# Decode attention of a two-layer decoder: softmax and values in two halves of four samples inside the prompt's heads

## The reference

```
def shared_kv(s, g, w_kv, b_f):
    z = rmsnorm(s, g) @ w_kv
    k = z[..., :SEQ_WIDTH].reshape(bsz, t, FOX_HEADS, HEAD_DIM)
    v = z[..., SEQ_WIDTH:2 * SEQ_WIDTH].reshape(bsz, t, FOX_HEADS, HEAD_DIM)
    logf = jax.nn.log_sigmoid(z[..., 2 * SEQ_WIDTH:].astype(F32) + b_f.astype(F32)).astype(s.dtype)
    return k, v, logf
...
def fox_block(q, k, v, cq, ck, qpos, kpos):
    s = jnp.einsum('bqhd,bkhd->bhqk', q, k).astype(F32) * ATTN_SCALE
    s = s + jnp.transpose(cq, (0, 2, 1))[..., None] - jnp.transpose(ck, (0, 2, 1))[:, :, None, :]
    s = jnp.where(mask, s, NEG_INF)
    p = jax.nn.softmax(s, axis=-1).astype(v.dtype)
    return jnp.einsum('bhqk,bkhd->bqhd', p, v)
...
def fox_sample(q, k_new, v_new, logf_new, k_past, v_past, logf_past):
    k = jnp.concatenate([k_past, k_new.astype(k_past.dtype)], axis=1)
    v = jnp.concatenate([v_past, v_new.astype(v_past.dtype)], axis=1)
    logf = jnp.concatenate([logf_past.astype(F32), logf_new.astype(F32)], axis=1)
    c = jnp.cumsum(logf, axis=1)
    return fox_block(q, k, v, c[:, past:], c, kpos[past:], kpos)
```

## Time and profile before

| | |
|---|---|
| median of 3 runs | 1623.56 us |
| lowest and highest | 1621.72 and 1624.8 us |
| the profiled execution | 1620.65 us |
| its span on the core | 1618.9 us |
| mean granted TensorE clock | 0.937 |
| PE busy | 1440.2 us (89%) |
| DVE, ACT, POOL busy | 983.1, 615.6, 671.6 us |

### The profile page before, as it was taken

How to read it: one execution, slowest core, us unless ns; L and a number is a source line. 1 busy time by engine, 2 the same in 40 slices (tenths; PEclk the granted TensorE clock), 3 DMA queues, 4 the chain that set the end, 5 groups by cost and what they waited for, 6 DMA issues and landing times.

```text
span 1618.9 us, 32326 instructions
## 1 busy us (share of the span) xinstructions
PE 1440.2 (89%) x12076; PEld 1331.4 (82%) x12076; DVE 983.1 (61%) x1553; ACT 615.6 (38%) x1004; POOL 671.6 (41%) x429
## 2 busy tenths in 40 slices
PE   7985597879998999999878979997979998999996
PEld 6974477879998999999777966644979998999996
DVE  5768826566775057763647468751577771277755
ACT  4552435245662133422332216520355551233312
POOL 0685421323343344442366769301414433344430
PEclk9997758999999999999898989997989999999998
DMA  5334452222323223333224746797212332233321
GB/s 168 120 92 80 84 153 77 66 66 79 81 80 93 83 88 91 96 92 84 75 81 142 207 151 201 234 373 249 85 46 78 90 93 83 73 90 92 109 78 58
DMA packets 288134, 180.42 MB, mean 111 GB/s; under 512 B 54072, under 2 KB 272860, under 8 KB 287980
## 3 DMA queue, kind: packets, MB, share of 16 engines
...
...
## 4 chain that ended last, share of the span: by engine, by line
PE 52%; DVE 17%; issue 16%; POOL 6%; ACT 4%; DVEq 1%; SPq 1%; DMA 1%; ACTq 0%; POOLq 0%
PE big L2414 42%; ACT yc L2279 3%; PE misc L2483 2%; PE misc L2469 2%; DVE rstd L1116 1%; PE big L2717 1%; DVE hf L1688 1%; POOL s5s L881 1%; DVE x_lo L1147 1%; DVE uc L1673 1%; DVE yc L1683 1%; DVE y L1605 1%; POOL e_tmp L881 1%; DVE yc L1680 1%; DVE tmp L1157 1%
## 5 line engine op out<-in xcount | busy, mean ns | idle before, releaser
L877 POOL TENSOR_TENSOR w_lo<-raw,w_hi 128x1024 fp32r<-128x1024 f32 (+2 forms) x163 | 423.0, 2595 | 787.9 <-ACT w_hi L1963 787.7
L2414 PE MATMUL big<-x_hi,w_hi 128*128 128x264 f32 (+1 forms) x2184 | 457.9, 292 | 41.2 <-DVE x_lo L1147 24.2
L2414 PE MATMUL big<-x_hi,w_lo 128*128 128x264 f32 (+1 forms) x2184 | 444.9, 285 | 0.0
L2414 PE MATMUL big<-x_lo,w_hi 128*128 128x264 f32 (+1 forms) x2184 | 443.7, 285 | 0.0
L1963 ACT ACTIVATE w_hi<-raw 128x1024 fp32r<-128x1024 f32 (+2 forms) x179 | 198.3, 1108 | 537.6 <-PE big L2414 497.9
L2414 PEld LDWEIGHTS big<-x_hi,w_hi 128*128 128x128 f32 x2184 | 342.4, 191 | 52.9 <-issue 44.2
L2414 PEld LDWEIGHTS big<-x_lo,w_hi 128*128 128x128 f32 x2184 | 340.9, 191 | 0.0
L2414 PEld LDWEIGHTS big<-x_hi,w_lo 128*128 128x128 f32 x2184 | 340.4, 191 | 0.0
L1677 DVE SCALAR_TENSOR_TENSOR yc<-uc,convw,yc 128x512 f32<-128x512 f32 x88 | 106.3, 1208 | 114.3 <-ACT yc L2279 114.3
L2414 PE MATMUL big<-h_hi,w_hi 128*128 128x264 f32 x704 | 144.7, 287 | 15.2 <-DVE h_lo L1692 12.0
L2414 PE MATMUL big<-h_lo,w_hi 128*128 128x264 f32 x704 | 143.0, 285 | 0.0
...
## 6 DMA issues: line engine op xcount, KB each, us to landing
...
areas<-in_cache_k SPq DMA_DIRECT2D x49, 384.0 KB, 4.1
areas<-in_cache_v SPq DMA_DIRECT2D x35, 384.0 KB, 6.2
...
extra<-in_cache_v SPq DMA_DIRECT2D x19, 384.0 KB, 5.3
...
```

What stands on the lines that cost most here:

```text
L877: pool.tensor_tensor(w_lo[slot][:, 0:kb, :], raw[slot][:, 0:kb, :], w_hi[slot][:, 0:kb, :].bitcast(F32), ALU.subtract).then_inc(lo_made, 1)
L2414: ins = pe.matmul(big[2 * slot + b_][:, 0:c1 - c0], w[slot][:, k, :], r[:, c0:c1], start=(k == 0 and n_ == 0), stop=(k == kb - 1 and n_ == 2))
```

## The change

1. **Two halves.** The scores, the sums of the softmax and the softmax itself are split into samples 0 to 3 and 4 to 7. The first half's softmax stands at steps 2 to 6, the second's at 30 to 34. The 16 pairs of pages of samples 0 to 3 have their value products one pair at a time, at steps 7, 8, 10, 12, 14, 15, 17, 19, 21, 22, 24, 26, 28, 29, 31 and 33. The value pages of samples 4 to 7 stay in the late part.
2. **Page order.** `page_loads` lets key and value pages take turns from the ninth key page after the thirtieth on. The key reductions are spread over 30 steps. The block of stores and mk still stands behind the last key page. mv moves back by eight value pages.
3. **Tables.** LOGF_AT, DECAY_AT from 1, 3 to 2, 4; K_FIRST (2, 3), one reduction of them ahead of the second norm; queries of samples 5, 6, 7 at steps 4, 12, 19.
4. **Log-forget chain.** One instruction in place of minus and min; the chain's second part (`log_forget`) stands behind kvT of panel 0, the scan, which now subtracts (`decay_row`), behind kvT of panel 1.
5. **POOL beside x's split.** Three key products ahead of the first w_lo; the fourth waits until x_lo is made.
6. **Masks.** `diagonal` stands after key product 31, its tiles in other memory.
7. `win1_queries`: the spreads of samples 0 and 1 move from the last slice of panel 6 to slices 0 and 2 of panel 7.

```diff
-Q_STEP = {5: 1, 6: 6, 7: 12}
-LOGF_AT, DECAY_AT = 1, 3
-K_STEP = 7 / 5
-K_FIRST = (3, 5)
-K_BEFORE_LO = (2, 5, 7, 9, 11, 13, 15, 17, 19, 21, 23, 25)
-K_BEHIND = K_BEFORE_LO[2:] + (27, 29)
-SOFT_AT = 25
-PV_AT = (30, 31, 32, 33, 34, 36, 38, 39)
-PV_BESIDE = len(PV_AT) // 2
+Q_STEP = {5: 4, 6: 12, 7: 19}
+LOGF_AT, DECAY_AT = 2, 4
+SPLITS_KV = 4 * KD + 3 * KS
+K_FIRST = (2, 3)
+K_BEFORE_LO = (3, 4, 6, 8, 10, 12, 14, 16, 18, 20, 22, 24)
+K_BEHIND = K_BEFORE_LO[2:] + (26, 28)
+SOFT_AT = (2, 30)
+PV_AT = tuple(7 + 7 * i // 4 for i in range(16))
+PV_BESIDE = len(PV_AT) // 4
...
+    early, ks, vs = (0, 1, 2, 3, KV_PAGE), (0, 1, 2, 3, AREAS[5]), AREAS[0:5]
+    out = [(n, early[n % 5]) for n in range(K_EARLY)]
+    nk, nv, turn = K_EARLY, 0, 0
+    while nk < NB * PAGES:
+        if nk < K_EARLY + 8 or turn:
+            out.append((nk, ks[(nk - K_EARLY) % 5]))
+            nk, turn = nk + 1, 0
+        else:
+            out.append((NB * PAGES + nv, vs[nv % 5]))
+            nv, turn = nv + 1, 1
...
 def scores_read(n):
-    return min(NB * PAGES, K_EARLY + int(K_STEP * n))
+    last = SOFT_AT[1]
+    return K_EARLY + min(n, last) * (NB * PAGES - K_EARLY) // last
...
-            for n in range(K_EARLY, v_at):
+            for n, _ in PAGE_LOADS[K_EARLY:LAST_KEYS + 1]:
                 page_load(n)
             for c in range(4):
                 store(O["prompt_v"][0, c * P:(c + 1) * P], vtok[:, c, :, 0:DH])
...
-            for n in range(v_at, 2 * NB * PAGES):
+            for n, _ in PAGE_LOADS[LAST_KEYS + 1:]:
                 page_load(n)
-                if n == 3 * NB * PAGES // 2:
+                if n == 13 * NB * PAGES // 8:
                     mem_v(1, mb[1])
...
                     for i in range(n):
+                        if i == 1:
+                            pool.wait_ge(s_("xlo_made"), SPLITS_KV)
                         k_products(K_BEFORE_LO[i - 1] if i else 0, K_BEFORE_LO[i])
                         lo(base + i, (base + i) % 2, kb)
-                    k_products(K_BEFORE_LO[n - 1], NB * PAGES)
+                    k_products(K_BEFORE_LO[n - 1], K_EARLY + 2)
                     diagonal()
+                    k_products(K_EARLY + 2, NB * PAGES)
...
-                tt(sc[0:NB, :, PAGES, :], idb, snew.unsqueeze(1).to_broadcast([NB, NB, HEADS]), ALU.mult)
-                tt(sc[0:NB, :, PAGES, :], sc[0:NB, :, PAGES, :], idneg.unsqueeze(2).to_broadcast([NB, NB, HEADS]), ALU.add)
+                for i in range(2):
+                    bs = slice(HALF_B * i, HALF_B * i + HALF_B)
+                    idb = ident[0:NB, bs].unsqueeze(2).to_broadcast([NB, HALF_B, HEADS])
+                    tt(sc[i][0:NB, :, PAGES, :], idb, snew.unsqueeze(1).to_broadcast([NB, HALF_B, HEADS]), ALU.mult)
+                    tt(sc[i][0:NB, :, PAGES, :], sc[i][0:NB, :, PAGES, :],
+                       idneg[:, bs].unsqueeze(2).to_broadcast([NB, HALF_B, HEADS]), ALU.add)
...
-            ts(m_, z_, -1.0, None, ALU.mult, ALU.bypass)
-            tell(V.tensor_tensor(m_, m_, z_, ALU.min), s_("nabs_ready"), 1)
-            dve.wait_ge(s_("log_made"), 1)
-            tell(V.scalar_tensor_tensor(m_, z_, 0.0, l_, ALU.min, ALU.subtract), s_("lf_ready"), 1)
-            sync()
-            do(V.memset(z_, 1.0))
-            sync()
-            do(V.tensor_tensor_scan(l_[:, 0:T], z_[:, 0:T], m_[:, 0:T], 0.0, ALU.mult, ALU.add))
-            sync()
-            do(V.tensor_scalar(lf[:, 0, 0:T], l_[:, 0:T], -1.0, None, ALU.mult, ALU.bypass))
+            tell(V.scalar_tensor_tensor(m_, z_, -1.0, z_, ALU.mult, ALU.min), s_("nabs_ready"), 1)
+
+            def log_forget():
+
+                dve.wait_ge(s_("log_made"), 1)
+                tell(V.scalar_tensor_tensor(m_, z_, 0.0, l_, ALU.min, ALU.subtract), s_("lf_ready"), 1)
+                sync()
+                do(V.memset(l_, 1.0))
+
+            def decay_row():
+
+                do(V.tensor_tensor_scan(z_[:, 0:T], l_[:, 0:T], m_[:, 0:T], 0.0, ALU.mult, ALU.subtract))
...
                 read_panel(q, lambda n, c0, c1: kvT[:, c0:c1])
                 sync()
                 mark(s_("kvT_ready"))
+                if m == 0:
+                    log_forget()
+                elif m == 1:
+                    decay_row()
                 k_scores(K_BEHIND[m])
```

More of the change, by code:

```diff
@@ L182, with page_loads @@
 Q_PANEL = {2: 2, 3: 5, 4: 9}
-Q_STEP = {5: 1, 6: 6, 7: 12}
-LOGF_AT, DECAY_AT = 1, 3
-K_STEP = 7 / 5
-K_FIRST = (3, 5)
-K_BEFORE_LO = (2, 5, 7, 9, 11, 13, 15, 17, 19, 21, 23, 25)
-K_BEHIND = K_BEFORE_LO[2:] + (27, 29)
-SOFT_AT = 25
-PV_AT = (30, 31, 32, 33, 34, 36, 38, 39)
-PV_BESIDE = len(PV_AT) // 2
-MQ_AT = 33
-def page_buffers():
-    early = [0, 1, 2, 3, KV_PAGE]
-    out = (early * NB * PAGES)[:K_EARLY]
-    late = [*AREAS, 0, 1, 2, 3]
-    out += (late * 4)[:NB * PAGES + len(late) - K_EARLY] + [QB_PAGE, *EXTRA]
-    last = {b: n for n, b in enumerate(out)}
-    pool = late + [QB_PAGE, *EXTRA]
-    kept = [b for b in pool if b not in AREAS]
-    while len(out) < 2 * NB * PAGES:
-        b = min(pool if len(out) < 2 * NB * PAGES - len(kept) else kept, key=lambda b: last[b])
-        last[b] = len(out)
-        out.append(b)
-    return out
-PAGE_BUFFER = page_buffers()
+Q_STEP = {5: 4, 6: 12, 7: 19}
[4 more added lines that the diff above has]
+K_BEHIND = K_BEFORE_LO[2:] + (26, 28)
+HALF_B = NB // 2
+SOFT_AT = (2, 30)
+PV_AT = tuple(7 + 7 * i // 4 for i in range(16))
+PV_BESIDE = len(PV_AT) // 4
+MQ_AT = 33
+def page_loads():
+    early, ks, vs = (0, 1, 2, 3, KV_PAGE), (0, 1, 2, 3, AREAS[5]), AREAS[0:5]
[8 more added lines that the diff above has]
+            nv, turn = nv + 1, 1
+    free = {b: i + (8 if n < NB * PAGES else 10) for i, (n, b) in enumerate(out)}
+    free.pop(KV_PAGE)
+    free.update({b: len(out) + 12 for b in (QB_PAGE, *EXTRA)})
+    kept = [b for b in free if b not in AREAS]
+    while nv < NB * PAGES:
+        b = min(free if nv < NB * PAGES - len(kept) else kept, key=lambda b: free[b])
+        free[b] = len(out) + 12
+        out.append((NB * PAGES + nv, b))
+        nv += 1
+    return out
+PAGE_LOADS = page_loads()
+PAGE_BUFFER = dict(PAGE_LOADS)
+LOADED_AT = {n: i for i, (n, _) in enumerate(PAGE_LOADS)}
+LAST_KEYS = LOADED_AT[NB * PAGES - 1]
 def pair_count(l, p):
@@ L240, in page_use @@
 def page_use(n):
-    return sum(page_buffer(i) == page_buffer(n) for i in range(n + 1))
+    return sum(b == page_buffer(n) for _, b in PAGE_LOADS[0:LOADED_AT[n] + 1])
 def page_in(n):
@@ L252, in page_before @@
 def page_before(n):
-    return max((i for i in range(n) if page_buffer(i) == page_buffer(n)), default=None)
+    return next((i for i, b in PAGE_LOADS[LOADED_AT[n] - 1::-1] if b == page_buffer(n)), None) if LOADED_AT[n] else None
 def fox_jobs():
@@ L262, in fox_jobs @@
         jobs += [("OT", 1, p) for p in LAST[1] if n == LAST[1][p] + 2]
-        jobs += [("fmaxT",)] * (n == SOFT_AT + 1) + [("fmax",)] * (n == SOFT_AT + 2) + [("fden",)] * (n == SOFT_AT + 4)
-        jobs += [("fpv", b) for b in range(PV_BESIDE) if n == PV_AT[2 * b + 1] + 1]
+        for i, at in enumerate(SOFT_AT):
+            jobs += [("fmaxT", i)] * (n == at + 1) + [("fmax", i)] * (n == at + 2) + [("fden", i)] * (n == at + 4)
+        jobs += [("fpv", b) for b in range(PV_BESIDE) if n == PV_AT[4 * b + 3] + 1]
         jobs += [("mq", 1, b) for b in range(NB) if n == MQ_AT + b]
@@ L1017, in diagonal @@
             def diagonal():
-                own.sync()
+                pool.wait_ge(s_("k_used"), K_EARLY)
                 own.do(pool.memset(block_diag, 0.0))
@@ L1793, in _ @@
                     mark(s_("qrow_ready"))
+                    k_scores(K_FIRST[0])
             sync()
@@ L2349, in _ @@
                     soft(1, n + 1)
-                if n == SOFT_AT + 3:
-                    decode_exp(sc, 2)
+                for i, at in enumerate(SOFT_AT):
+                    if n == at + 3:
+                        decode_exp(sc[i], 2 + i)
                 if n < NBANKS[1]:
@@ L2883, in _ @@
                 product(base + m, (base + m) % 2, kb, xs_, HALF, x_split if m == 0 else None,
-                        each=first if m == 0 else win1_queries if m == 6 else None)
+                        each={0: first, 6: win1_queries, 7: spread_queries}.get(m))
             nsplit[0] += KD
@@ L3010, in _ @@
             for b in range(PV_BESIDE + 2, NB):
-                pv(2 * b)
-                pv(2 * b + 1)
+                for pair in range(4):
+                    pv(4 * b + pair)
                 pv_sum(b)
```

197 lines of the change are left out of this document (104 added, 93 removed).

## The result

| | before | changed |
|---|---|---|
| median (4 runs each) | 1623.28 us | 1637.39 us |
| lowest and highest | 1621.72, 1624.8 | 1633.4, 1641.52 |
| profiled execution | 1620.65 | 1639.11 |
| span | 1618.9 | 1637.4 |

The ratio is 1.0087 with an interval of 1.0058 to 1.0116: slower by about 14 us. A second set of runs of the changed kernel gave 1.009 (1.0065 to 1.0114) beside the kernel before.

What follows compares the result with a forecast made beforehand. PE was taken as the bound nearly everywhere, the queues from 1050 us on. The front's −7.55 and the heads' +10.15, late part included, gave +2.6: 1623.25 by the profile, 1626 by the median, range 1610 to 1640.

Steps and rivals of the forecast that it cites:

- the stores in the way: Rival A, the forecast itself: stores delay value pages in the heads, the front's gain is spent; 1619 to 1634, chance 0.50.
- rival C: Heads: pages land in 6.2 us instead of 3.9, six late pairs wait 3 us each; 1640, chance 0.18.
- the wait at step 29: Heads: PE waits 11.0 us for value page V27 behind the stores and mk, bounds 4 and 13.
- split of x: Ahead of the heads: log-forget panel takes 9.5 us instead of 11.8, −2.3, between 0 and −5.
- PE's wait and slow third panel: Ahead of the heads: the 6.81 us idle before the third key panel goes, −6.8, and its slow start, −1.3.
- ring: Ahead of the heads: five jobs fall behind one panel, the fifth has the first's bank; +1.4, between 0 and 3.6.
- front in all: Everything ahead of the heads, gains and amounts given back together: −7.55, between −11 and −3.
- V7: Heads: PE's old wait of 1.25 us for the first page behind the stores goes, −1.25.
- small waits: Heads: four waits of 1.0 us for value pages of samples 0 to 3, +4, between 0 and 16.
- softmax waits: Heads: two halves wait 0.8 and 1.2 in place of 1.78; with the cold stretch gone, net −0.9.
- slow clock and added work in the heads: Heads: PE runs cold after the 11.0 us wait for a value page, +1.3.
- late part: After the steps: 17 value pages left to load instead of 23, at 1.19 us each; −7, between −8 and −2.

Runs made afterwards that it cites:

- a_block_lead: The changed kernel with the edits of a_block_late and value pages taking turns two key pages sooner; median 1615.58 us, ratio 0.9960 to the kernel before.
- a_block_late: The changed kernel with the memory's keys loaded behind value page 31 and the six stores behind value page 41; median 1629.44 us, ratio 1.0066 to the kernel before.

## Why the forecast was near in mechanism and short in size

I had said 1626 with a range of 1610 to 1640 and 0.43 for slower; it is 1637.4, slower. The likeliest case, the stores in the way, is what happened, but the time lies above that case's own range, 1619 to 1634. It is inside the whole range only because that reached up to rival C's 1640, and C's cause, pages that land slowly, did not occur in the steps: this part is luck. By the signs I had named the mechanism stands: the wait at step 29 is 12.5 (between 5 and 14), and the first scores came 7.0 us sooner (between 4 and 11).

By the steps of the sum, measured on the profiled executions:

| step | forecast | measured |
|---|---|---|
| split of x | −2.3 | −4.5 (11.8 to 7.3) |
| spreads of samples 0 and 1 | −0.75 | −0.7 (27.2 to 26.5 from 816.82 and 819.05 to the log-forget panel) |
| PE's wait and slow third panel | −8.1 | both gone |
| new_scores | +2.2 | +1.9 (4.85 for 2.92) |
| ring | +1.4 | +2.8 (2.43, and 1.76 for 1.38) |
| front in all | −7.55 | −9.3 from 816.82 and 819.05 on |
| wait at the pair of step 29 | +11.0 | +12.5 |
| V7 | −1.25 | gone |
| small waits | +4 | +8.0 |
| softmax waits | +0.2 | +0.3 (1.75 and 0.33 for 1.78) |
| memory queries | +3 | +3.1 (6.2 for 3.1) |
| slow clock and added work in the heads | +0.2 | +7.9 |
| late part | −7 | −5.2 |
| in all | +2.6 | +16.5 (the medians: +14.1) |

The forecast's softmax term of −0.9 and its 1.3 of slow clock are split here into waits (+0.2) and the rest (+0.2).

- **The wait behind the stores** was right in place, cause and nearly in size: 23.1 behind the start of step 26 was the forecast; step 26 began at 1044.59 and the page was used at 1070.76, 26.2. K63 went out 5.8 after it instead of 3.9: the reduction of K58 ended at 1048.0, 3.4 after it, but SP was behind by then, with K62 at 1047.93 and V25 at 1049.29 still to issue ahead of K63. PE's own way there was added up as 12.1; its parts, 4 × 2.28, 1.5 and 1.66, make 12.3, and the wait by them 10.8.
- **"I take four waits of 1.0"** was mis-sized. The six pairs that the tables name waited, and one more: 1.99, 1.12, 0.17, 2.23, 0.92, 0.72, 0.86, 8.0 instead of 4, still far from C's 18. The landing time was not at fault, 3.9 to 4.1 as taken. I had worked the margin out for one page and used it for all. The fit of the Trainium skill ("DMA: Bandwidth & Descriptors", section "Anatomy of one DMA") is given there for DMAs that GpSimd issues; these are SyncE's. Used for them all the same, it would be 2.9 us by estimate and no wait; the trace has 3.9 to 4.1 and seven waits.
- **The clock** was the term that failed most: I gave the 11 us wait 1.3 us of slow clock. After 12.5 idle PE ran at 1.2 GHz from 1070.76 to about 1081, two steps and a softmax turn, and again around 1095 and from 1109 on. The 10.4 us behind the wait are some 5 us of lost time, by an estimate from the two clocks. Of the 7.9 us of added busy time, a_block_lead has 1.2, with the waits gone and the clock at 0.98. So 6.7 us are the clock's. They can't be put down to the long wait alone: a_block_late, without it, has the same busy time, 127.0, and only with the small waits gone too does it fall to 120.5.
- **The front** came out near the forecast, −9.3 for −7.55, by terms that missed in opposite directions: kvf was better since the clock rose after 3.5 us (pairs of 0.64 until 849.0, then 0.40), where I had kept it low for six and a half slices, and the ring was worse by 1.4.
- **The late part** began with every buffer full, as forecast, and then loaded 17 pages; it took 31.4 instead of 29.6. That wins nothing on its own: in 1105 to 1115 the queues stood empty (0 to 2 GB/s), while PE, which has to free the buffers, waits in the memory queries.
